# Chunk inverse of an RWKV-7 / forgetting-attention decoder layer: 104-wide products against packed 64-wide quarters of TensorE

## The chip, the cores and the metric

The kernel runs on one core of a Trainium2 chip. The metric is device time in microseconds for one execution. The kernel before took 2462.89 us, the median of three runs (2462.32 to 2469.64).

## What is computed

One decoder layer over 1040 prompt positions (16 learned ones and 1024 given) and 8 sample rows. The part that matters here is the scan of the time mixing, for 8 heads of width 64:

```python
def wkv_scan(r, decay, k, v, kk, a, state0):
    def step(state, inp):
        r_t, w_t, k_t, v_t, kk_t, a_t = inp
        s_kk = jnp.einsum('bhvk,bhk->bhv', state, kk_t)
        state = (state * w_t[:, :, None, :]
                 - s_kk[..., None] * (kk_t * a_t)[:, :, None, :]
                 + v_t[..., None] * k_t[:, :, None, :])
        return state, jnp.einsum('bhvk,bhk->bhv', state, r_t)
...
def decoder_layer(x, shift_prev, wkv0, attend, lw):
    h = rms_norm(x, lw['norm_mix'])
    u = h @ lw['w_in']
    u_r, u_f, u_g = jnp.split(u, [D_SHIFT, D_SHIFT + D_FOX_IN], axis=-1)
    o_r, new_shift, new_wkv = rwkv_time_mix(u_r, shift_prev, wkv0, lw)
    ...
    o_f = attend(q, k, v, lf)
    g_r, g_f = jnp.split(u_g, 2, axis=-1)
    merged = jax.nn.sigmoid(g_r) * (o_r @ lw['w_br_rwkv']) + jax.nn.sigmoid(g_f) * (o_f @ lw['w_br_fox'])
    x = x + merged @ lw['w_out']
    x = x + jnp.square(jax.nn.relu(rms_norm(x, lw['norm_ffn']) @ lw['w_ffn_up'])) @ lw['w_ffn_down']
```

All arithmetic is in fp32, some of the large products in two fp32r parts.

## The kernel before

The program runs these stages one after another: the projection for the time mixing (14 tiles of 128 columns), the preparation of the scan's operands, the chunk loop (314 to 1066 us), the rest of the fillers, attention, the branch and output projections, and the MLP with 2 x 32 column tiles.

The scan is done in 10 chunks of C = 104 positions, one pass of the chunk loop each, for 8 heads at once. Within a chunk the recurrence is solved by the inverse of a unit triangular 104 x 104 matrix for each head. `MB` holds the products of the chunk, masked; the inverse is built in place by doubling. Level 0 gives I - B0, where B0 is the part of `MB` between positions 2i and 2i+1; at level lv, blocks of 2^lv positions are joined into blocks of 2^(lv+1): with X the inverse so far and B the part of `MB` between the two blocks, X becomes X - X B X. The kernel holds X (`Xm`) and its transpose (`XTr`), since both stand as an operand. There are N_LV = 7 levels, 0 to 6; level 6 joins the positions below 64 to those above.

By engine, within a pass:

- GpSimd (L1935 to L1941) makes `bm_lv`, the mask of level lv times `MB`, for all heads in one operation (104 x 832), into the two buffers of `Bm` in turn.
- VectorE makes `xt_init` (L1601), the identity minus `Bm[0]`.
- TensorE transposes `XTr` (L890) into banks 0 and 1, four heads each (q = 0, 1), and ScalarE copies the result to `Xm` (L1313).
- In each level 1 to 6, for q = 0 and then q = 1: TensorE multiplies `Bm` with `Xm` (t1, L902, banks 0 and 1), ScalarE copies the result to `T1` (L1320), TensorE multiplies `XTr` with `T1` for the new `Xm` (t2, L913, banks 2 and 3; not in level 6) and `T1` with `XTr` for the new transpose (t2, L915, banks 4 and 5), and VectorE subtracts both from PSUM (L1611, L1613).
- Then TensorE goes on with `wt` (L924), `u` (L943, L947), `y` (L951, L954, L959) and the state (L963, L966), all with `XTr` or what follows from it. VectorE normalises, TensorE transposes the result (L972), and the next pass begins.

Each engine runs its own instructions in the order in which they are written; they meet in counting semaphores (`ch_pe`, `ch_act`, `ch_dve`, `ch_pool`), one step for each named result. `Filler` (L345) puts products of the later projections between these: a pass does 48 of 128 x 128 x 350, and `fill.run(n)` issues the next n of them. In each level one stands behind t1 and one behind t2, and `fill.run(2)` stands behind level 6. An fp32 matmul leaves two records in the trace, each with a weight load (LDWEIGHTS) of its own; a transpose leaves one.

The names that the change touches are `Xm`, `XTr`, `T1`, `Bm` (tiles at L492 to L497), the step lists `ch_dve` and `ch_pool` (L515, L520), and the bodies of the chunk on TensorE (L887 to L943), ScalarE (L1311 to L1320), VectorE (L1564, L1600 to L1614) and GpSimd (L1934 to L1941).

Of the kernel before, what the change touches and what calls it, by code (L numbers as in the profile page):

```python
# [129 lines left out]
def build(nc, A):  # L130
    with ExitStack() as ctx:
# [290 lines left out]
        for u in range(N_UN):  # L422
# [9 lines left out]
            if a + 1 == HN and i + 1 < HP:  # L432
# [59 lines left out]
        Xm, XTr = r_ch.take(NH, C), r_ch.take(NH, C)  # L492
# [3 lines left out]
        T1 = r_c2.take(NH, C)  # L496
        Bm = r_c2.take(NH, C), r_c2.take(NH, C)  # L497
# [20 lines left out]
                          for t in (("x", "xt") if lv < N_LV - 1 else ("xt",))]  # L518
                       + ["sum", "mean", "state_sum", "state", "center", "sq", "var", "norm"])
        ch_pool = Steps(sem("ch_pool"), [f"bm_{lv}" for lv in range(N_LV)] + ["bonus", "gate"])  # L520
# [254 lines left out]
        def _(pe):  # L775
# [59 lines left out]
            def pe_chunk(c):  # L835
# [17 lines left out]

                fill.run(16)
# [33 lines left out]
                for q in range(2):  # L888
                    for j in range(4):
                        last = pe.transpose(PS[0:C, q, j * C:(j + 1) * C], XTr[0:C, 4 * q + j], ident[0:C, 0:C])  # L890
                    ch_pe.done(last, f"x_{q}")
                for lv in LEVELS:
                    for q in range(2):
                        if q == 0:
                            pe.wait_ge(ch_pool.sem, ch_pool.after(c, f"bm_{lv}"))
# [24 lines left out]
                fill.run(2)  # L920
                wait(ch_dve, f"x_{N_LV - 1}_1_xt")
                for h in range(NH):
                    e, p = h // HP, h % HP
                    last = pe.matmul(PS[e * HD:(e + 1) * HD, 0, p * C:(p + 1) * C], An[0:C, vcols(h)],  # L924
                                     XTr[0:C, h], start=True, stop=True)
# [16 lines left out]
                for h, e, p, rows in by_rows():  # L942
                    pe.matmul(u_out(e, p), XTr[0:C, h], Zm[0:C, h * HD:(h + 1) * HD], start=(p == 0), stop=False,  # L943
# [1140 lines left out]
```

## Time and profile before

| | before |
|---|---|
| median of three runs | 2462.89 us |
| the profiled execution | 2458.04 us |
| its span, first to last instruction | 2456.2 us |
| mean granted TensorE clock | 0.972 of full |
| busy: TensorE, VectorE, ScalarE, GpSimd | 92, 38, 23, 8% |
| the chunk loop | ten passes of 74.95 us |

A row of a profile names a line of the kernel, an engine (PE is TensorE, PEld its weight loads, DVE VectorE, ACT ScalarE, POOL GpSimd, SP the engine that issues transfers), the operation and its tiles. Matmuls are pipelined: the time of one record overlaps the next, so a rate is read from starts, not from the length of one record.

### The profile page before, as it was taken

To read this page: it belongs to the slowest core of one execution; us is meant where nothing else is said; L and a number is where in the kernel's file an instruction comes from. 1 tells how busy PE (TensorE), PEld (TensorE's weight loads), DVE (VectorE), ACT (ScalarE), POOL (GpSimd) and SP (SyncE) were. 2 spreads that over 40 slices of the span, in tenths; PEclk is the share of its full clock that TensorE was granted. 3 is DMA by queue.
4 is the path that set the end of the run, shared out by engine and by line. 5 is a ranking of instruction groups with operands and counts; after the bars stand their busy time and mean duration, and the time that the engine had idled before them with its cause. 6 is when DMAs were issued, how large, how long until landed. Compare 5 with 4: busy or idle time off the path is not lost.

```text
span 2456.2 us, 37471 instructions
## 1 busy us (share of the span) xinstructions
PE 2251.5 (92%) x14718; PEld 1880.7 (77%) x14718; DVE 936.9 (38%) x1400; ACT 577.0 (23%) x913; POOL 191.0 (8%) x136
## 2 busy tenths in 40 slices
PE   2998689999999999999888899996999999999995
PEld 1996377778777788765555566666999999999995
DVE  5332644433444433433467622116322222222234
ACT  3112422222222222231334322003211211211220
POOL 0000022112221122200111000000000000000000
PEclk8999899999999999999899999998999999999998
DMA  2114621100111111156553634211111111111111
GB/s 110 44 43 109 179 85 46 45 33 13 45 45 55 46 35 45 42 142 115 193 182 124 210 118 177 78 34 43 43 52 43 43 47 47 43 43 51 43 43 70
DMA packets 108390, 184.31 MB, mean 75 GB/s; under 512 B 65070, under 2 KB 65390, under 8 KB 104966
## 3 DMA queue, kind: packets, MB, share of 16 engines
q1 hardware_dynamic: 106022, 174.95, 22.8%
q10 hardware_dynamic: 2304, 8.50, 1.4%
q8 instruction: 41, 0.67, 0.1%
q14 instruction: 23, 0.19, 0.0%
HBM read 147.71 MB, written 35.71 MB: 75 GB/s over the span
## 4 chain that ended last, share of the span: by engine, by line
PE 86%; DVE 9%; ACT 2%; issue 2%; DMA 1%; SPq 0%; ACTq 0%; DVEq 0%
PE ps L279 36%; PE ps L345 16%; PE ps L255 9%; PE ps L902 4%; PE ps L915 4%; PE ps L913 3%; PE ps L1153 2%; DVE arena L1730 2%; PE ps L1138 1%; PE ps L1125 1%; DVE arena L1596 1%; PE ps L874 1%; DVE normed L327 1%; PE ps L843 1%; PE ps L954 1%
## 5 line engine op out<-in xcount | busy, mean ns | idle before, releaser
L345 PE MATMUL ps<-normed,weights 128*128 128x350 f32 x1344 | 440.0, 468 | 8.4 <-ACTq L1265 8.3
L279 PE MATMUL ps<-h_split,w_split 128*128 128x350 f32 x2304 | 375.9, 325 | 14.7 <-DVE h_split L1883 14.7
L279 PEld LDWEIGHTS ps<-h_split,w_split 128*128 128x128 f32 x2304 | 374.0, 191 | 16.9 <-issue 12.9
L279 PE MATMUL ps<-ff_split,w_split 128*128 128x350 f32 x2304 | 371.4, 323 | 0.0
L279 PEld LDWEIGHTS ps<-ff_split,w_split 128*128 128x128 f32 x2304 | 370.9, 189 | 0.0
L345 PEld LDWEIGHTS ps<-normed,weights 128*128 128x128 f32 x1344 | 243.7, 192 | 121.3 <-issue 10.0
L1870 DVE TENSOR_TENSOR arena<-arena,ps 128x1050 f32 (+1 forms) x40 | 50.0, 1249 | 351.9 <-PE ps L279 266.5
L1941 POOL TENSOR_TENSOR arena<-arena,constants 104x832 f32<-104x832 f32 x70 | 136.2, 1952 | 580.6 <-DVE arena L1596 444.9
L255 PE MATMUL ps<-fox,weights 128*128 128x350 f32 x576 | 171.3, 457 | 3.0 <-DVE fox L1860 3.0
L255 PEld LDWEIGHTS ps<-fox,weights 128*128 128x128 f32 x576 | 109.0, 189 | 64.0 <-issue 3.6
L915 PE MATMUL ps<-arena 104*104 104x104 f32 x960 | 155.0, 255 | 0.0
L289 ACT CAST w_split<-weights 128x1024 fp32r<-128x1024 f32 x78 | 81.4, 1043 | 275.9 <-PE ps L279 245.1
L279 PE MATMUL ps<-h_high,w_split 128*128 128x350 f32 x672 | 129.5, 327 | 16.7 <-DVE h_low L1481 16.7
L913 PE MATMUL ps<-arena 104*104 104x104 f32 x800 | 138.6, 255 | 0.0
L1899 DVE TENSOR_TENSOR squares<-squares 128x1050 f32<-128x1050 f32 x32 | 40.1, 1254 | 248.5 <-ACT squares L1449 248.5
L1611 DVE TENSOR_TENSOR arena<-arena,ps 104x416 f32<-104x416 f32 x100 | 58.7, 587 | 189.5 <-PE ps L915 189.5
L279 PEld LDWEIGHTS ps<-h_high,w_split 128*128 128x128 f32 x672 | 113.0, 191 | 18.8 <-issue 13.7
L293 DVE TENSOR_TENSOR w_split<-weights,w_split 128x1024 fp32r<-128x1024 f32 x78 | 95.1, 1220 | 82.5 <-ACT w_split L289 82.5
L915 PEld LDWEIGHTS ps<-arena 104*104 104x104 f32 x960 | 121.7, 172 | 2.3
L913 PEld LDWEIGHTS ps<-arena 104*104 104x104 f32 x800 | 109.4, 172 | 11.4
L902 PEld LDWEIGHTS ps<-arena 104*104 104x104 f32 x960 | 100.4, 171 | 22.2 <-ACT arena L1313 4.5
L902 PE MATMUL ps<-arena 104*104 104x104 f32 x960 | 108.7, 260 | 2.4 <-ACT arena L1313 2.4
(255 smaller groups left out, 2314.4 us busy)
## 6 DMA issues: line engine op xcount, KB each, us to landing
weights<-in_wu SPq DMA_DIRECT2D x122, 512.0 KB, 3.5
normed<-in_vp SPq DMA_DIRECT2D x64, 260.0 KB, 4.8
normed<-in_kp SPq DMA_DIRECT2D x64, 256.0 KB, 5.3
arena<-chunk_dram SPq DMA_DIRECT2D x10, 1248.0 KB, 5.5
arena<-gate_dram SPq DMA_DIRECT2D x16, 525.0 KB, 4.7
chunk_dram<-arena SPq DMA_DIRECT2D x12, 520.0 KB, 6.7
chunk_dram<-fox SPq DMA_DIRECT2D x12, 520.0 KB, 4.2
arena<-samp_dram SPq DMA_DIRECT2D x10, 512.0 KB, 9.3
```

What stands on the lines that cost most here:

```text
L255: last = pe.matmul(PS[:, 3 * s + g, 0:G], W[:, s, k * P:(k + 1) * P], x[:, k, g * G:(g + 1) * G], start=(k == 0), stop=(k == nk - 1))
L279: last = pe.matmul(PS[:, 3 * s + g, 0:G], ws[:, s, wh, k * P:(k + 1) * P], x[xh][:, k, g * G:(g + 1) * G], start=(k == 0 and wh + xh == 0) ...
L289: act.copy(of[0][:, s, 0], W[:, s]).then_inc(w_hi[s], 1)
L293: dve.tensor_tensor(of[0][:, s, 1], W[:, s], of[0][:, s, 0], ALU.subtract).then_inc(w_split[s], 1)
L345: last = self.pe.matmul(PS[:, 6 + m % 2, 0:G], W[:, s, k * P:(k + 1) * P], HT[:, k, g * G:(g + 1) * G], start=(k == 0), stop=(k == KT - 1))
L902: last = pe.matmul(PS[0:C, q, j * C:(j + 1) * C], Bm[lv % 2][0:C, h], Xm[0:C, h], start=True, stop=True)
L913: pe.matmul(PS[0:C, 2 + q, j * C:(j + 1) * C], XTr[0:C, h], T1[0:C, h], start=True, stop=True)
L915: last = pe.matmul(PS[0:C, 4 + q, j * C:(j + 1) * C], T1[0:C, h], XTr[0:C, h], start=True, stop=True)
L1153: last = pe.matmul(PS[e * HD:(e + 1) * HD, 6, at:at + C], vnat[0:C, b, col:col + HD], PTm[0:C, u % 2, e, s0 + b], start=(b == 0), stop=(b ...
L1611: done(dve.tensor_tensor(quad(Xm, q), quad(Xm, q), PS[0:C, 2 + q, 0:4 * C], ALU.subtract), f"x_{lv}_{q}_x")
L1870: dve.tensor_tensor(dst, dst, grp(s), ALU.add).then_inc(evac[s], 1)
L1941: ch_pool.done(pool.tensor_tensor(Bm[lv % 2][0:C], MB[0:C, :, 0], mask, ALU.mult), f"bm_{lv}")
```

## The change

Each head's 104 x 104 matrices are kept as two diagonal blocks: positions 0 to 63 on partitions 0 to 63 (`top`), positions 64 to 103 on partitions 64 to 103 (`low`), both in 64 columns. The levels 1 to 5 never couple the two, so each product is made as two products of 64 rows, one on the first and one on the last quarter of TensorE's array. Level 6 makes only the block between them. The full transpose is put together in a new tile `XTF` by the last two levels. The transposes of `XTr` become products with a packed identity.

```diff
-        Xm, XTr = r_ch.take(NH, C), r_ch.take(NH, C)
+        HB, HR = 64, C - 64
+        Xm, XTr, XTF = r_ch.take(NH, HB), r_ch.take(NH, HB), r_ch.take(NH, C)
...
+        identP = r_c2.take(HB)
+        top, low = slice(0, HB), slice(HB, C)
+        half_turn = sem("half_turn")
...
+                def by_halves(bank, j, lhs, rhs, h=None):
+                    at = slice(j * HB, (j + 1) * HB)
+                    a = lhs[:, (bank % 2) * 4 + j]
+                    b = rhs if h is None else rhs[:, h]
+                    pe.matmul(PS[top, bank, at], a[top], b[top], start=True, stop=True)
+                    return pe.matmul(PS[low, bank, at], a[low, 0:HR], b[low], start=True, stop=True)
...
                 for q in range(2):
+                    if q == 0:
+                        pe.sem_inc(half_turn, 1)
                     for j in range(4):
-                        last = pe.transpose(PS[0:C, q, j * C:(j + 1) * C], XTr[0:C, 4 * q + j], ident[0:C, 0:C])
+                        last = by_halves(q, j, XTr, identP)
                     ch_pe.done(last, f"x_{q}")
-                for lv in LEVELS:
+                for lv in LEVELS[:-1]:
                     for q in range(2):
...
+                        pe.sem_inc(half_turn, 1)
                         for j in range(4):
-                            h = 4 * q + j
-                            last = pe.matmul(PS[0:C, q, j * C:(j + 1) * C], Bm[lv % 2][0:C, h], Xm[0:C, h],
-                                             start=True, stop=True)
+                            last = by_halves(q, j, Bm[lv % 2], Xm, 4 * q + j)
                         ch_pe.done(last, f"t1_{lv}_{q}")
                     fill.run(1)
                     for q in range(2):
                         wait(ch_act, f"t1_{lv}_{q}")
...
+                        pe.sem_inc(half_turn, 1)
                         for j in range(4):
                             h = 4 * q + j
-                            if lv < N_LV - 1:
-                                pe.matmul(PS[0:C, 2 + q, j * C:(j + 1) * C], XTr[0:C, h], T1[0:C, h],
+                            if lv < N_LV - 2:
+                                by_halves(2 + q, j, XTr, T1, h)
+                            else:
+                                pe.matmul(PS[top, 2 + q, j * HB:(j + 1) * HB], XTr[top, h], T1[top, h],
                                           start=True, stop=True)
-                            last = pe.matmul(PS[0:C, 4 + q, j * C:(j + 1) * C], T1[0:C, h], XTr[0:C, h],
-                                             start=True, stop=True)
+                        for j in range(4):
+                            last = by_halves(4 + q, j, T1, XTr, 4 * q + j)
                         ch_pe.done(last, f"t2_{lv}_{q}")
                     fill.run(1)
+                lv = N_LV - 1
+                for q in range(2):
+                    wait(ch_dve, f"x_{lv - 1}_{q}_x")
+                    pe.sem_inc(half_turn, 1)
+                    for j in range(4):
+                        h = 4 * q + j
+                        last = pe.matmul(PS[low, q, j * HB:(j + 1) * HB], MB[top, h, 0, low], Xm[top, h],
+                                         start=True, stop=True)
+                    ch_pe.done(last, f"t1_{lv}_{q}")
+                fill.run(1)
+                for q in range(2):
+                    wait(ch_act, f"t1_{lv}_{q}")
+                    wait(ch_dve, f"x_{lv - 1}_{q}_xl")
+                    pe.sem_inc(half_turn, 1)
+                    for j in range(4):
+                        h = 4 * q + j
+                        last = pe.matmul(PS[top, 4 + q, j * HB:j * HB + HR], T1[low, h], XTF[low, h, low],
+                                         start=True, stop=True)
+                    ch_pe.done(last, f"t2_{lv}_{q}")
+                fill.run(1)
 
                 fill.run(2)
...
-                        ch_act.done(act.copy(quad(T1, q), PS[0:C, q, 0:4 * C]), f"t1_{lv}_{q}")
+                        part = slice(0, C) if lv < N_LV - 1 else low
+                        ch_act.done(act.copy(quad(T1, q)[part], PS[part, q, 0:4 * HB]), f"t1_{lv}_{q}")
...
+            for b in Bm:
+                order(dve.memset(b[low, :, HR:HB], 0.0))
+            order(dve.memset(XTF[low, :, top], 0.0))
+            order(dve.tensor_copy(identP[top], ident[top, 0:HB]))
+            order(dve.tensor_copy(identP[low], ident[low, HB:2 * HB]))
...
                         if lv < N_LV - 1:
-                            done(dve.tensor_tensor(quad(Xm, q), quad(Xm, q), PS[0:C, 2 + q, 0:4 * C],
+                            part = slice(0, C) if lv < N_LV - 2 else top
+                            done(dve.tensor_tensor(quad(Xm, q)[part], quad(Xm, q)[part], PS[part, 2 + q, 0:4 * HB],
                                                    ALU.subtract), f"x_{lv}_{q}_x")
-                        done(dve.tensor_tensor(quad(XTr, q), quad(XTr, q), PS[0:C, 4 + q, 0:4 * C],
-                                               ALU.subtract), f"x_{lv}_{q}_xt")
+                        if lv < N_LV - 2:
+                            done(dve.tensor_tensor(quad(XTr, q), quad(XTr, q), PS[0:C, 4 + q, 0:4 * HB],
+                                                   ALU.subtract), f"x_{lv}_{q}_xt")
+                        elif lv < N_LV - 1:
+                            done(dve.tensor_tensor(XTF[top, four, top], XTr[top, four], moved(4, top, HB),
+                                                   ALU.subtract), f"x_{lv}_{q}_xt")
+                            done(dve.tensor_tensor(XTF[low, four, low], XTr[low, four, 0:HR], moved(4, low, HR),
+                                                   ALU.subtract), f"x_{lv}_{q}_xl")
+                        else:
+                            done(dve.tensor_scalar(XTF[top, four, low], moved(4, top, HR), -1.0, None, ALU.mult),
+                                 f"x_{lv}_{q}_xt")
...
-                for lv in range(N_LV):
+                for lv in range(N_LV - 1):
...
+                    for part, name in ((top, "top"), (low, "low")):
+                        n = part.stop - part.start
+                        mask = cst[part, C_LV + lv * C + part.start:C_LV + lv * C + part.stop]
+                        ch_pool.done(pool.tensor_tensor(Bm[lv % 2][part, :, 0:n], MB[part, :, 0, part],
+                                                        mask.unsqueeze(1).to_broadcast([n, NH, n]), ALU.mult),
+                                     f"bm_{lv}_{name}")
+                        pool.wait_ge(ch_pool.sem, ch_pool.after(c, f"bm_{lv}_{name}"))
```

The products `wt` and `u` read `XTF` in place of `XTr`, with the same shapes. `moved(bank, part, n)` names the first n of 64 columns of each of four heads in PSUM.

## Rows read from the trace of the kernel before

**Rows 1.** The page: busy time by engine, and the chain that ended last.

```profile
PE 2251.5 (92%) x14718; PEld 1880.7 (77%) x14718; DVE 936.9 (38%) x1400; ACT 577.0 (23%) x913; POOL 191.0 (8%) x136
...
PE 86%; DVE 9%; ACT 2%; issue 2%; DMA 1%; SPq 0%; ACTq 0%; DVEq 0%
PE ps L279 36%; PE ps L345 16%; PE ps L255 9%; PE ps L902 4%; PE ps L915 4%; PE ps L913 3%; PE ps L1153 2%; DVE arena L1730 2%; PE ps L1138 1%; PE ps L1125 1%; DVE arena L1596 1%; PE ps L874 1%; DVE normed L327 1%; PE ps L843 1%; PE ps L954 1%
```

**Rows 2.** Table by stretch: busy us (xinstructions) by engine, then granted clock, DMA share, GB/s.

```profile
690.85:765.80 74.95, 72.59 (x569) 58.42 (x567) 30.80 (x46) 18.45 (x37) 16.17 (x9) 0.98 0.11 31
713.72:749.45 35.73, 35.49 (x310) 31.23 (x309) 12.90 (x22) 7.79 (x16) 9.70 (x5) 1.00 0.04 15
...
1198.00:1400.00 202.00, 170.94 (x1713) 107.10 (x1713) 143.44 (x475) 83.55 (x207) 26.12 (x38) 0.94 0.50 169
```

**Rows 3.** Waits of TensorE, 390 to 1066 us: us in total, times, longest.

```profile
PE ps L972 <- DVE arena L1642: 18.1, 9, 2.0
...
PE ps L902 <- ACT arena L1313: 2.1, 9, 0.2
```

**Rows 4.** Chain of waits inside one level: start us, us, what.

```profile
726.52 1.67 PE ps L902 x16
728.19 0.61 PE ps L345 x2
...
731.73 0.32 PE ps L345
```

**Rows 5.** Timeline of TensorE behind the levels: start us, us, instructions.

```profile
747.57 1.95 PE L345 MATMUL ps<-normed,weights 128*128 128x350 f32 x6
749.45 1.34 PE L924 MATMUL ps<-arena 104*64 104x104 f32 x16
750.72 1.44 PE L345 MATMUL ps<-normed,weights 128*128 128x350 f32 x4
752.00 1.60 PE L943 MATMUL ps<-arena 104*104 104x64 f32 x16
753.53 0.95 PE L947 MATMUL ps<-arena 64*104 64x64 f32 x16
754.31 0.90 PE L951 MATMUL ps<-arena 64*104 64x64 f32 x16
...
759.41 0.69 PE L963 MATMUL ps<-arena 104*64 104x64 f32 x16
759.93 0.64 PE L966 MATMUL ps<-arena 104*64 104x64 f32 x16
```

**Rows 6.** Timeline: VectorE and ScalarE around one level, and two operations for size.

```profile
702.10 0.59 ACT L1302 COPY arena<-ps 104x512 f32<-104x512 f32 x1
...
725.75 0.78 PE L345 MATMUL ps<-normed,weights 128*128 128x350 f32 x2
725.95 0.59 DVE L1611 TENSOR_TENSOR arena<-arena,ps 104x416 f32<-104x416 f32 x1 [0.26 <-PE ps L915]
...
727.36 0.51 ACT L1320 COPY arena<-ps 104x416 f32<-104x416 f32 x1 [4.38 <-PE ps L902]
...
760.61 0.42 DVE L1634 TENSOR_TENSOR arena<-arena,ps 128x256 f32<-128x256 f32 x1 [0.19 <-PE ps L966]
```

**Rows 7.** Timeline where the first copy begins: GpSimd, VectorE, TensorE.

```profile
708.86 3.85 POOL L1941 TENSOR_TENSOR arena<-arena,constants 104x832 f32<-104x832 f32 x2 [13.47 <-DVE arena L1596]
...
710.83 2.75 DVE L1601 TENSOR_TENSOR arena<-constants,arena 104x832 f32<-104x832 f32 x1 [2.06 <-POOL arena L1941]
...
713.72 0.88 PE L890 MATMUL ps<-constants,arena 104*104 104x104 f32 x8
```

**Rows 8.** Timeline before the first pass: VectorE.

```profile
319.39 1.60 DVE L1578 TENSOR_TENSOR_SCAN arena<-constants,arena 128x104 f32<-128x104 f32 x4 [4.92 <-DMA arena<-chunk_dram]
```

**Rows 9.** DMA from 300 to 765 us: one queue's packets and MB; one issue's us to landing.

```profile
q8 instruction: 5, 0.08, 0.1%
...
lora_weights<-in_vp SPq DMA_DIRECT2D x48, 4.0 KB, 1.7
```

More of the change, by code:

```diff
@@ L495, in build @@
         MB = r_c2.take(NH, 2, C)
-        T1 = r_c2.take(NH, C)
-        Bm = r_c2.take(NH, C), r_c2.take(NH, C)
+        T1 = r_c2.take(NH, HB)
+        Bm = r_c2.take(NH, HB), r_c2.take(NH, HB)
+        identP = r_c2.take(HB)
+        top, low = slice(0, HB), slice(HB, C)
+        half_turn = sem("half_turn")
         Zm = r_c2.take(512)
@@ L517, in build @@
                        + [f"x_{lv}_{q}_{t}" for lv in LEVELS for q in range(2)
-                          for t in (("x", "xt") if lv < N_LV - 1 else ("xt",))]
+                          for t in (("x", "xt") if lv < N_LV - 2 else ("x", "xt", "xl") if lv < N_LV - 1 else ("xt",))]
                        + ["sum", "mean", "state_sum", "state", "center", "sq", "var", "norm"])
-        ch_pool = Steps(sem("ch_pool"), [f"bm_{lv}" for lv in range(N_LV)] + ["bonus", "gate"])
+        ch_pool = Steps(sem("ch_pool"), [f"bm_{lv}_{b}" for lv in range(N_LV - 1) for b in ("top", "low")] + ["bonus", "gate"])
         ds_pe, ds_act, ds_dve = sem("ds_pe"), sem("ds_act"), sem("ds_dve")
@@ L888, in pe_chunk @@
                 for q in range(2):
+                    if q == 0:
+                        pe.sem_inc(half_turn, 1)
                     for j in range(4):
-                        last = pe.transpose(PS[0:C, q, j * C:(j + 1) * C], XTr[0:C, 4 * q + j], ident[0:C, 0:C])
+                        last = by_halves(q, j, XTr, identP)
                     ch_pe.done(last, f"x_{q}")
-                for lv in LEVELS:
+                for lv in LEVELS[:-1]:
                     for q in range(2):
                         if q == 0:
-                            pe.wait_ge(ch_pool.sem, ch_pool.after(c, f"bm_{lv}"))
+                            pe.wait_ge(ch_pool.sem, ch_pool.after(c, f"bm_{lv}_low"))
                         if lv == 1:
@@ L924, in pe_chunk @@
                     last = pe.matmul(PS[e * HD:(e + 1) * HD, 0, p * C:(p + 1) * C], An[0:C, vcols(h)],
-                                     XTr[0:C, h], start=True, stop=True)
+                                     XTF[0:C, h], start=True, stop=True)
                 ch_pe.done(last, "wt")
@@ L942, in pe_chunk @@
                 for h, e, p, rows in by_rows():
-                    pe.matmul(u_out(e, p), XTr[0:C, h], Zm[0:C, h * HD:(h + 1) * HD], start=(p == 0), stop=False,
+                    pe.matmul(u_out(e, p), XTF[0:C, h], Zm[0:C, h * HD:(h + 1) * HD], start=(p == 0), stop=False,
                               skip_group_check=True)
@@ L1312, in act_chunk @@
                     wait(ch_pe, f"x_{q}")
-                    ch_act.done(act.copy(quad(Xm, q), PS[0:C, q, 0:4 * C]), f"x_{q}")
+                    ch_act.done(act.copy(quad(Xm, q), PS[0:C, q, 0:4 * HB]), f"x_{q}")
                 out(2)
@@ L1599, in _ @@
                             cm, ALU.mult), f"mask_{m}{i}")
-                wait(ch_pool, "bm_0")
-                done(dve.tensor_tensor(XTr[0:C], ident[0:C, 0:C].unsqueeze(1).to_broadcast([C, NH, C]),
+                wait(ch_pool, "bm_0_low")
+                done(dve.tensor_tensor(XTr[0:C], identP[0:C].unsqueeze(1).to_broadcast([C, NH, HB]),
                                        Bm[0][0:C], ALU.subtract), "xt_init")
@@ L1609, in _, with moved @@
                         wait(ch_pe, f"t2_{lv}_{q}")
+                        four = slice(4 * q, 4 * q + 4)
+                        def moved(bank, part, n):
+                            return PS[part, bank + q, 0:4 * HB].rearrange("p (a b) -> p a b", a=4)[:, :, 0:n]
                         if lv < N_LV - 1:
-                            done(dve.tensor_tensor(quad(Xm, q), quad(Xm, q), PS[0:C, 2 + q, 0:4 * C],
+                            part = slice(0, C) if lv < N_LV - 2 else top
+                            done(dve.tensor_tensor(quad(Xm, q)[part], quad(Xm, q)[part], PS[part, 2 + q, 0:4 * HB],
                                                    ALU.subtract), f"x_{lv}_{q}_x")
-                        done(dve.tensor_tensor(quad(XTr, q), quad(XTr, q), PS[0:C, 4 + q, 0:4 * C],
-                                               ALU.subtract), f"x_{lv}_{q}_xt")
+                        if lv < N_LV - 2:
[9 more added lines that the diff above has]
+                                 f"x_{lv}_{q}_xt")
                 def heads(ap):
@@ L1939, in _ @@
                         pool.wait_ge(ch_pe.sem, ch_pe.after(c, f"t1_{lv - 2}_1"))
-                    mask = cst[0:C, C_LV + lv * C:C_LV + (lv + 1) * C].unsqueeze(1).to_broadcast([C, NH, C])
-                    ch_pool.done(pool.tensor_tensor(Bm[lv % 2][0:C], MB[0:C, :, 0], mask, ALU.mult), f"bm_{lv}")
+                    for part, name in ((top, "top"), (low, "low")):
[5 more added lines that the diff above has]
+                        pool.wait_ge(ch_pool.sem, ch_pool.after(c, f"bm_{lv}_{name}"))
                 pool.wait_ge(bg_in, 16 * c + 16)
```

## The prediction

> **What bounds the kernel now.** I read the page first: of the span of 2456.2 us TensorE is busy for 92%, and of the chain that ended last 86% is TensorE; VectorE, ScalarE and GpSimd have long idle times [rows 1]. The three product lines of the chunk inverse, L902, L913 and L915, stand in that chain with 4 + 4 + 3%, some 260 us. Then the table by stretch: one pass of the chunk loop takes 74.95 us, and the stretch that the change rewrites, from the transposes of `XTr` to the `wt` products, takes 35.73 us, in which TensorE is busy for 35.49 at full granted clock [rows 2]. Then TensorE's waits over nine passes: apart from the 2 us before the last transposes of each pass it waits for almost nobody, 2.1 us in all in front of L902 [rows 3]. So in this stretch the stream of TensorE's instructions is the bound, and what is taken from the stream is taken from the time, until a wait shows.
>
> The chain of one level shows how the 5.82 us of a level are made [rows 4]: 1.67 us for the sixteen records of the t1 products (an fp32 matmul leaves two records), 0.61 for one filler matmul, then 32 records of the t2 products, from 728.80 to the next filler at 731.73, one filler more. The t2 records come every 2.93 / 32 = 92 ns, which is 0.88 ns for each of their 104 moving columns. The t1 records come every 104 ns; sixteen at 92 would be 1.47, so 0.2 us of each level is waiting already, for VectorE's two subtractions (below).
>
> The stretch holds 14 filler matmuls (2 for each of six levels, then `fill.run(2)`) at 0.61, together 8.5 us. What is the inverse's own is 35.7 - 8.5 = **27.2 us**.
>
> **The change, step by step.**
>
> *Records.* Before: 8 transposes with one record each, 96 of t1 and 176 of t2, 280 in a pass. After: each 104-wide product is two 64-wide ones. The first copy becomes 16 products (32 records); t1 in levels 1 to 5 is 5 x 16 products (160); t2 in levels 1 to 4 is 4 x 32 products (256); in level 5 it is 8 + 16 products (48); level 6 is 8 + 8 products (32). That is 528 records, of which 48 (the eight of level 5 that make only the top block, and all of level 6) lie on one quarter of the array; the other 480 alternate between two quarters.
>
> *What a quarter record costs.* No row shows a 64 x 64 tile. The nearest are in the tail of the pass [rows 5]. L963 has 64-column weights in alternating column halves and 64 moving columns: 16 records from 759.41 to 759.93, 33 ns each. L947 has alternating row halves, but 104-column weights: 16 records from 753.53 to 754.31, 49 ns. L943, full width, 104-column weights and only 64 moving columns: 1.53 / 16 = 96 ns, no less than with 104 moving columns. So loading the 104 columns takes as long as moving 104, and it is the larger of the two that sets the pace: 0.88 x 104 / 2 = 46 explains L947's 49, and 0.88 x 64 / 2 = 28 explains L963's 33. A diagonal quarter has 64 columns on both sides and differs from its neighbour in rows and columns, so it is nearest to L963: I take **33 ns**, with 30 and 50 (L947) as ends. A record on one quarter alone has no partner: 0.88 x 64 = 57 ns. 480 x 33 + 48 x 57 = 15.8 + 2.7 = 18.5 us in place of the old records.
>
> *Changes between full width and quarters.* Each filler matmul is now surrounded by quarters: 25 changes in a pass, before there were none inside a level. L924 shows both directions [rows 5]: six filler records of 302 ns from 747.57 would end at 749.38 and L924 begins at 749.45; the four fillers behind it take 1.28 instead of 1.21. So 0.07 a change, 1.7 us. Ends 0 and 0.15 (the weights of the next tile are not loaded ahead, one load is exposed).
>
> *The 25 increments of `half_turn`.* As I read the code, the wait in front of a group of quarters now sits on an instruction of the queue and not on the first product. Where the wait is over before the queue gets there they are hidden by the filler in the queue. Where it binds (the q = 1 group of t1 in each level, the two first groups of level 1, about 8 in a pass) the restart costs one more step; the trace of before has no such increment inside the stretch, the nearest is VectorE's end at 713.58 to TensorE's start at 713.72 [rows 7], so up to 0.14 each and I take 0.1: 0.8 us. Ends 0 and 25 x 0.14 = 3.5.
>
> *The waits inside a level.* t2 of q = 1 ends, 0.2 later VectorE starts (the filler behind t2 begins at 725.75, the subtraction at 725.95 [rows 6]), now two subtractions of 256 columns; 0.42 each by L1634 [rows 6] instead of 0.59, together 0.87 with the gap, then 0.14 back to TensorE: 1.21 us. Its cover is one filler and the q = 0 group of t1: 0.61 + 16 x 0.033 = 1.14. So 0.1 us of stall in each of five levels, where there was 0.2. ScalarE's copy of 256 columns (0.37, by 0.51 for 416 and 0.59 for 512 [rows 6]) has filler plus 0.5 us as cover. In level 1 the shorter groups expose the copies of x_0 and x_1 by some 0.2. Sum 0.7 us.
>
> *The last level.* It is a chain of small steps: t2 of level 5, VectorE (now three operations for each q, 0.42 + 0.42 + 0.32), t1 (0.46 for each q), copy, t2 (0.46 each), one operation, `wt`. I followed it: t1 of q = 1 is ready to start 2.99 us after the start of level 5's t2 and TensorE is at it at 3.04; its copy is back at 4.20 while TensorE has to do q = 0's t2 until 4.56; VectorE's last result is ready at 5.7 and the `wt` products come at 6.8, behind three fillers. Nothing is exposed, and 1.1 us of cover is left at the end.
>
> *GpSimd and the start of the stretch.* Masking goes in two pieces of 64 and 40 rows: (512 + 320) columns at 1.95 / 832 us [rows 7] are again 1.95, plus 0.1 or so for the wait between. `xt_init` shrinks from 2.76 to about 1.7. It ended at 713.58, just when TensorE was at its end of the fillers; it will end 0.8 us earlier. The other masks have a level (4.8 us) for 2.1 us of work. Cost nothing.
>
> *Setup.* Three memsets and two copies on VectorE before the loop, about 1.3 us. There VectorE waits 4.92 us for the first chunk to land [rows 8]. Cost nothing; without that cover 1.3 us once.
>
> *Sum for a pass.* 18.5 + 1.7 + 0.8 + 0.7 = **21.7 us** in place of 27.2: 5.5 us less, the stretch falls from 35.7 to 30.2, the pass from 75.0 to 69.4, a middle level from 5.8 to about 4.8. Nothing else in the pass changes: fillers, `wt`, tail. The weights for the fillers and the next chunk land 3 to 6 us after their issue and the pass stays far longer than that. Ten passes: 55 us. The profiled execution took 2458.04 us, 4.85 under the median of 2462.89; 2458 - 55 = 2403 for it, and from the median **2408 us**.
>
> **The rivals.**
>
> *A: the changes and increments cost nothing.* 18.5 + 0.5 us a pass, 8.2 less: 2381. For it: L924's 0.07 may be rounding of the modelled starts. 13%.
>
> *B: waits take over.* The margins in a level are 0.1 us; if each step of VectorE, ScalarE or the restart of the queue is a little longer than I take it, half a microsecond a level is exposed: 3 us a pass, gain 2.5: 2438. For it: TensorE already stalled 0.2 us a level at the slower pace. 12%.
>
> *C: the loop no longer stays in TensorE's instruction memory.* A pass has 572 records now, each with a weight load of its own, 820 after. The trace shows five fetches of instructions on queue q8 from 300 to 765 us, through six passes [rows 9]: the first pass fetches, the others run from memory. If the longer body falls out, each of the eight jumps back waits for a fetch; a small transfer takes 1.7 us to land [rows 9]. 14 us more: 2422. Against it: at the jump TensorE waits 2.0 us for VectorE anyway [rows 3], and that would hide most. 8%.
> The Trainium skill (Runtime: NRT & Kernel Launch, Instruction fetch mechanics) gives TensorE room for 2048 instructions in pages of 256. By that page 2 x 820 matmul instructions with their loads, and some 80 waits and register operations, lie over eight pages, all that there are, with none for the page ahead; by it C would come true. The trace agrees as far as the pages go: five packets are 0.08 MB, 16 KB each [rows 9].
>
> *D, the slower side: quarters that share a bank run one after another, or load as slowly as row halves.* Top and low quarter of a product write the same bank, which L947's row halves do not; L963's column halves do. The point from which the change loses is (27.2 - 2.7 - 3.2) / 480 = **44 ns** a record. At L947's 49 to 50 ns the pass is 2.7 us longer: 2490 (8%, of which 2 lie within 0.3% of no change, at 43 to 46 ns). Fully in turn, at 57 ns: 480 x 57 = 27.4, and 33.3 us a pass in place of 27.2: 2524 (4%).
> The Trainium skill (TensorEngine Tiling (Array Packing), Restrictions and Gotchas) says that different row tiles cannot access the same PSUM bank simultaneously. Read strictly, that page gives the 57 ns and the sum of 2524; L963 agrees only in that column tiles of one bank do overlap.
>
> *E: half the array idle lets the granted clock fall* from 2.4 to 1.2 GHz, and TensorE's 27 us of the new stretch double: 2408 + 270 = 2678. Against it: the attention stage, with its small tiles and 85% busy, was granted 0.94 [rows 2]. 2%.
>
> **How the numbers follow.** The forecast has 53%: 2395 to 2423, its own spread from 31 to 35 ns and 0 to 0.1 a change. A 13, B 12, C 8, D 12, E 2. A measurement of this kernel can tell about 0.3%, 7 us, from no change. Faster: 53 + 13 + 12 + 8 = 86%. Within: 2%. Slower: 6 + 4 + 2 = 12%. The range leaves out D and E (14%) and some tails: 2378 to 2446.
>
> **What would show it.** In the trace of after: the period between the t1 groups of levels 2 to 4 (5.82 before) at 4.6 to 5.0 us; sixteen records of a q group in 0.53 us; chunk starts 69.4 us apart; TensorE's waits in front of the t1 line under 0.2 us each. D shows as a group of 16 records taking 0.8 us or more, B as waits for VectorE or ScalarE inside the levels, C as more than five q8 packets in the six passes of the first loop and a gap at its head, E in the granted clock. I am wrong in the main if a quarter record costs over 44 ns, or if the 25 restarts cost far over 0.1 us each.

## The result, and the profile after

| | before | after |
|---|---|---|
| median (lowest to highest) | 2462.32 us (2456.48 to 2469.64) | 2449.17 us (2446.01 to 2450.52) |
| the profiled execution | 2458.04 us | 2450.52 us |
| its span | 2456.2 us | 2448.7 us |

The ratio of the times is 0.9944, with a 95% interval of 0.9927 to 0.9960: 13 us faster, where 55 us were forecast, and 3 us above the upper end of the forecast range. What follows shows that the change itself gained 67 us and that 54 of them were lost again at a place it doesn't touch.

The table by stretch of the kernel after, in the columns of [rows 2]: one pass of the chunk loop, the stretch from the first product with the packed identity to `wt`, one middle level, and the last pass of the first loop:

```profile
389.00:463.56 74.56, 68.29 (x820) 50.32 (x821) 25.83 (x49) 16.70 (x37) 15.72 (x15) 0.96 0.14 39
413.40:442.80 29.40, 29.30 (x558) 22.10 (x559) 9.67 (x24) 6.00 (x16) 8.50 (x8) 1.00 0.07 20
418.47:423.12 4.65, 4.65 (x101) 3.54 (x101) 1.68 (x4) 0.74 (x2) 2.12 (x2) 1.00 0.02 4
688.41:759.90 71.49, 68.77 (x820) 50.52 (x821) 22.78 (x43) 13.53 (x29) 14.23 (x13) 0.96 0.13 38
```

The stretch is where the change was made, and it fell from 35.7 us to 29.4 (30.2 was forecast), a middle level from 5.8 us to 4.65. Yet the pass is 74.56 us and was 74.95 [rows 2]. TensorE is busy 68.29 of them, so over 6 us are idle, and its granted clock is 0.96 and not 0.98. Inside the stretch the clock is 1.00. The loss is outside the stretch.

The waits of TensorE from 390 to 1056 us, in the columns of [rows 3]:

```profile
PE ps L345 <- issue: 28.9, 7, 5.0
PE ps L1009 <- DVE arena L1700: 18.1, 9, 2.0
PE ps L886 <- DVE arena L1639: 5.5, 18, 0.4
```

The second and third row are the old waits (L1009 is the transpose of the result, L972 before). The first is new: seven times TensorE waits for nothing that the profile shows, in front of a filler product (an eighth such wait lies ahead of 390 us). The chain of waits at two jumps from the end of a pass to the head of the next, and at the place where the first loop falls through to the second without a jump:

```profile
458.69 0.70 DVE arena L1700
...
459.44 0.58 PE ps L1009 x4
460.02 3.54 issue
...
759.33 0.58 PE ps L1009 x4
759.90 2.32 PE ps L345 x7
...
827.88 0.57 PE ps L1009 x4
828.46 4.97 issue
833.42 11.80 PE ps L345 x32
```

All eight jumps back have such a gap: 3.63, 3.54, 3.63, 3.59 and 3.53 us in the first loop, 4.97, 4.99 and 4.60 in the second, 32.5 us together. The fall-through has none. Nor does the kernel before have one at its jumps: L972 ends there at 390.77 and the next filler starts at 390.80.

```profile
390.19 0.58 PE L972 MATMUL ps<-constants,arena 104*128 104x104 f32 x4 [2.02 <-DVE arena L1642]
390.80 9.68 PE L345 MATMUL ps<-normed,weights 128*128 128x350 f32 x32
```

The page and the transfers of 300 to 757 us count the packets that fetch instructions:

```profile
q8 instruction: 117, 1.92, 0.3%
...
q8 instruction: 52, 0.85, 0.8%
```

117 in the whole run, where the kernel before has 41, and 52 in the first loop, where it has five [rows 9]. The transfers inside the first gap alone, 385.37 to 389.00 us:

```profile
q8 instruction: 1, 0.02, 2.2%
```

Each of the eight gaps holds one such packet of 16 KB. By narrower windows it starts at 386.00 here, 0.6 us after the transposes, and takes 1.3 us (2.2% of 16 engines' 3.63 us); TensorE starts 1.7 us after its end, and the next packet begins at 389.48, when TensorE is already running. In the second loop the packet starts 1.9 to 2.3 us after the transposes, and that makes those gaps the longer ones.

The gap costs more than its length. The timeline of TensorE's weight loads and products around the first jump:

```profile
384.79 0.38 PEld L1009 LDWEIGHTS ps<-constants,arena 104*128 104x128 f32 x4 [2.56 <-DVE arena L1700]
388.99 0.50 PEld L345 LDWEIGHTS ps<-normed,weights 128*128 128x128 f32 x2 [3.83 <-issue]
389.74 0.34 PEld L345 LDWEIGHTS ps<-normed,weights 128*128 128x128 f32 x1 [0.25 <-issue]
390.32 0.34 PEld L345 LDWEIGHTS ps<-normed,weights 128*128 128x128 f32 x1 [0.24 <-issue]
```

and the table by stretch of the head's 32 filler records:

```profile
389.00:394.00 5.00, 5.00 (x9) 3.03 (x10) 2.38 (x4) 0.00 (x0) 0.88 (x1) 0.50 0.26 51
394.00:401.14 7.14, 7.14 (x27) 4.55 (x26) 0.00 (x0) 0.45 (x1) 0.00 (x0) 1.00 0.61 209
```

Two idle stretches stand close together, 2.0 us for VectorE and then 3.6 us for instructions, and after them the granted clock is 0.50, the lower of its two levels (1.2 GHz): filler records stand 0.58 us apart and not 0.29. The 32 records take 12.14 us where they take 9.44 at full clock (experiment 1). The eight heads take 97.1 us together (11.5 to 12.6 each), which is 21.6 us more than eight of 9.44. Gaps and heads together: 32.5 + 21.6 = 54.1 us.

### The profile page after: what moved, and what is told of

Same layout as the page of the kernel before. It is cut to its first block, busy times and chain, and to the rows that moved or that the text cites. A ratio compares the mean times of both kernels' runs of the same rounds, so it can differ in the third digit from the quotient of the medians.

```text
span 2448.7 us, 42896 instructions
## 1 busy us (share of the span) xinstructions
PE 2208.9 (90%) x17198; PEld 1796.3 (73%) x17198; DVE 884.7 (36%) x1425; ACT 559.1 (23%) x913; POOL 187.6 (8%) x186
## 4 chain that ended last, share of the span: by engine, by line
PE 84%; DVE 9%; issue 3%; DMA 1%; ACT 1%; SPq 0%; ACTq 0%; DVEq 0%
PE ps L279 36%; PE ps L345 17%; PE ps L255 9%; PE ps L863 4%; PE ps L864 3%; PE ps L1190 2%; DVE arena L1788 2%; PE ps L1175 1%; PE ps L1162 1%; DVE arena L1639 1%; PE ps L886 1%; PE ps L847 1%; PE ps L991 1%; DMA weights<-in_wu 1%; PE ps L811 1%
## 5 line engine op out<-in xcount | busy, mean ns | idle before, releaser
L345 PE MATMUL ps<-normed,weights 128*128 128x350 f32 x1344 | 468.1, 491 | 43.9 <-issue 32.5
L279 PEld LDWEIGHTS ps<-h_split,w_split 128*128 128x128 f32 x2304 | 372.1, 190 | 18.7 <-issue 12.9
L345 PEld LDWEIGHTS ps<-normed,weights 128*128 128x128 f32 x1344 | 252.5, 199 | 173.9 <-issue 58.9
L863 PEld LDWEIGHTS ps<-arena 64*64 64x64 f32 x2400 | 148.6, 135 | 46.1 <-issue 46.1
L2001 POOL TENSOR_TENSOR arena<-arena,constants 64x512 f32<-64x512 f32 x120 | 132.5, 1104 | 553.5 <-DVE arena L1639 496.9
L863 PE MATMUL ps<-arena 64*64 64x64 f32 x2400 | 163.7, 220 | 1.0
L864 PE MATMUL ps<-arena 40*40 40x64 f32 x2400 | 157.9, 218 | 0.0
L864 PEld LDWEIGHTS ps<-arena 40*40 40x40 f32 x2400 | 139.2, 112 | 0.0
L1660 DVE TENSOR_TENSOR arena<-arena,ps 104x256 f32<-104x256 f32 (+1 forms) x100 | 41.9, 419 | 180.1 <-PE ps L864 173.9
L1788 DVE CUSTOM_DVE_ANT_0 arena<-ps,arena 104x416 f32<-104x416 f32 (+3 forms) x152 | 67.8, 493 | 83.8 <-PE ps L1162 83.8
L1487 ACT ACTIVATE squares<-ps 128x1050 f32<-128x1050 f32 x32 | 33.5, 1048 | 259.5 <-PE ps L279 259.5
```

Of the source, the lines that this page charges most:

```text
L279: last = pe.matmul(PS[:, 3 * s + g, 0:G], ws[:, s, wh, k * P:(k + 1) * P], x[xh][:, k, g * G:(g + 1) * G], start=(k == 0 and wh + xh == 0) ...
L345: last = self.pe.matmul(PS[:, 6 + m % 2, 0:G], W[:, s, k * P:(k + 1) * P], HT[:, k, g * G:(g + 1) * G], start=(k == 0), stop=(k == KT - 1))
L863: pe.matmul(PS[top, bank, at], a[top], b[top], start=True, stop=True)
L864: return pe.matmul(PS[low, bank, at], a[low, 0:HR], b[low], start=True, stop=True)
L1660: done(dve.tensor_tensor(quad(Xm, q)[part], quad(Xm, q)[part], PS[part, 2 + q, 0:4 * HB], ALU.subtract), f"x_{lv}_{q}_x")
L1788: dve.tensor_tensor_reduce(Sm[u % 3][0:C, e, lo:hi].rearrange("p b t -> p (b t)"), PS[0:C, 2 * (n % 2) + e, (lo - CUTS[c][0]) * C:(hi - CU ...
```

## Experiments

All ratios are to the kernel before, which ran on the same chip beside each of them.

**1 and 2. No jumps, after and before.** TensorE's two loops are written out, so that its stream has no jump. Nothing else changes:

```diff
-            with pe.Fori(0, C_FOX) as c:
-                pe_chunk(c)
-            with pe.Fori(C_FOX, NC) as c:
-                pe_chunk(c)
+            for c in range(NC):
+                pe_chunk(c)
```

> The kernel after, with TensorE's ten passes of the chunk written out one behind the other and no jump back; the work is the same. Theory F (fetch): the gap of 3.5 to 5.0 us at the head of eight passes, and the first fillers that run at the lower clock behind it (12.3 instead of 9.7 us), come from the jump back to instructions that have to be fetched again. Written out there is no jump: no gap, passes of 68 to 69 us, 2449 - 8 x 6.3 = about 2399 us, ratio to before 0.975. Rival L (the gap is a wait of the loop's end, such as draining TensorE or a transfer, or belongs to the quarters): the gap stays, and the time stays within 10 us of 2449.

> The kernel before with TensorE's passes written out in the same way. Theory F: its loop ran from instruction memory without a gap, so nothing is won: within 0.3% of 2462, passes of 75 us. If writing out helps by itself (its waits are against constants, with 56 register operations fewer in a pass), this kernel too is faster, by up to 50 us, and e1 would not show the fetch.

The kernel after without jumps: 2394.61 us, ratio 0.9726 (0.9704 to 0.9749). That is 54.6 us under the looped one, and 54.1 were counted in the trace. One pass of it, and the chain at the head of this pass:

```profile
452.60:520.92 68.32, 65.64 (x821) 48.98 (x821) 25.93 (x48) 16.68 (x37) 15.81 (x14) 1.00 0.14 42
```

```profile
452.02 0.57 PE ps L1009 x4
452.60 9.44 PE ps L345 x32
```

No gap, full clock, a pass of 68.32 us. The looped pass is this one plus its gap and its slow head: 68.32 + 3.54 + (12.14 - 9.44) = 74.56, the measured length of the first looped pass. The kernel before without jumps: 2461.44 us, ratio 0.9997 (0.9985 to 1.0009). Its jumps cost nothing, so the 54 us are not the price of jumps as such. Instruction packets alone don't decide either: written out, the kernel after fetches 96 packets and the one before 76, and neither waits for them. A stream that goes straight on is fetched ahead, a jump is not.

**3. Half the jumps.** Two passes to a turn of the loop: three jumps in place of eight, bodies twice as long.

```diff
-            with pe.Fori(0, C_FOX) as c:
-                pe_chunk(c)
+            with pe.Fori(0, C_FOX // 2) as c:
+                pe_chunk(2 * c)
+                pe_chunk(2 * c + 1)
...
```

> The kernel after with two passes in each turn of TensorE's loops: three jumps back instead of eight. Theory F: three gaps, each about as long as before, 2449 - 5 x 6.3 = about 2418 us. Rival L, if the gap belongs to each pass: 2449; if it grows with the length of the body: gaps of 7 us or more and no gain.

2413.34 us, ratio 0.9805 (0.9782 to 0.9828). Its waits have `PE ps L345 <- issue: 11.7, 3, 5.0`, and the chain at the first of the three jumps:

```profile
454.62 0.57 PE ps L1009 x4
455.19 3.51 issue
458.70 12.05 PE ps L345 x32
```

So each jump has its price, 3.2 to 5.0 us of gap and over 2 us of slow head, and three of them cost 18.7 us (2413.34 - 2394.61).

**4, 8, 9 and 10. The kernel before with a longer body.** Does length alone bring the gaps, without quarters and without `half_turn`? One-element products whose result is unused stand in front of the transposes of `yt`; all else is computed as before. A pass of TensorE has 1200 instructions before and 1722 after (an fp32 matmul is four: two records and their two weight loads).

```diff
+                for _ in range(133):
+                    pe.matmul(PS[0:1, 4, 0:1], ident[0:1, 0:1], ident[0:1, 0:1], start=True, stop=True)
                 wait(ch_dve, "norm")
```

> The kernel before with 133 matmuls of one element (266 records, 532 instructions) added ahead of the last transposes of each pass, which makes its loop as long as that of the kernel after. Theory F: gaps of 3.5 to 5 us at the head of eight passes and over 100 packets on q8, as in the kernel after, without any quarter. Rival L (the quarters or the increments cause the gap): no gap, 41 packets. The added matmuls themselves cost some 5 to 8 us a pass either way.

> The kernel before with 62 matmuls of one element in a pass (124 records, 248 instructions; e4 had 532). The loop is then about 1450 instructions long. Theory F with room for eight pages of 256, one of them for the page ahead: the loop lies over seven and stays, no gap, five packets on q8 from 300 to 765 us as before. If the room is smaller, gaps of 2.4 us and more as in e4.

> The kernel before with 85 matmuls of one element in a pass (170 records, 340 instructions, a loop of about 1540). The first loop begins some 3.8 pages of 256 instructions into TensorE's program (by the moments of the first fetches) and ends at 9.8: seven pages. Theory F with room for eight pages, one of them ahead: it stays, no gap, and so does the second loop (9.8 to 15.8). Rival: the limit is by length and under 1540: gaps at the head of both loops' passes.

> The same with 110 (220 records, 440 instructions, a loop of about 1640). The first loop goes from page 3.8 to 10.2, eight pages; the second from 10.2 to 16.6, seven pages. Theory F with whole pages: gaps at the five jumps of the first loop, none at the three of the second. Rival (the length alone decides): all eight jumps alike, with or without a gap.

| added matmuls | instructions in a pass | gaps in the first loop (5 jumps) | in the second (3) | instruction packets |
|---|---|---|---|---|
| 0 | 1200 | none | none | 41 |
| 62 | about 1450 | none | none | 43 |
| 85 | about 1540 | none | none | 43 |
| 110 | about 1640 | all, 3.55 to 3.83 us | none | 89 |
| 133 | about 1732 | all, 2.4 to 2.9 us | all, 3.0 to 3.4 us | 117 |

Length brings the gaps without any quarter: with 133 added products the kernel before has the gaps and the very 117 packets of the kernel after. (Each of the four ran once; their times hold the added products too and are not compared.) The run with 110 is the telling one: the same body waits in one loop and not in the other. The first of its gaps in the chain, and its waits:

```profile
395.11 0.88 PE ps L974 x4
395.99 3.55 issue
```

```profile
PE ps L345 <- issue: 18.5, 5, 3.8
```

The packets are 16 KB, 256 instructions [rows 9]. If the memory holds whole pages of them, what counts is how many a loop touches, and that depends on where it starts. By the moments of the first fetches the first loop starts near page 3.8 (an estimate; counted in this way, experiments 9 to 11 come out only for a start at 0.75 to 0.98 of a page). With 110 products a pass is 6.4 pages: the first loop then lies from 3.8 to 10.2 and touches eight, the second from 10.2 to 16.6 and touches seven. Eight wait, seven don't. The same counting gives seven for both loops with 85 products (6.0 pages), and eight for both with 133 (6.8) and in the kernel after (6.7). The place of a loop's start alone doesn't decide either: both loops of experiment 9 start near 0.8 of a page, as the first of experiment 10 does, and have no gap.

**11. The kernel after with its loops shifted.** This is the test that could have refuted it. The bodies, all 1722 instructions of them, stay as they are:

```diff
+            for _ in range(16):
+                pe.matmul(PS[0:1, 4, 0:1], ident[0:1, 0:1], ident[0:1, 0:1], start=True, stop=True)
             with pe.Fori(0, C_FOX) as c:
                 pe_chunk(c)
+            for _ in range(19):
+                pe.matmul(PS[0:1, 4, 0:1], ident[0:1, 0:1], ident[0:1, 0:1], start=True, stop=True)
             with pe.Fori(C_FOX, NC) as c:
                 pe_chunk(c)
```

> The changed kernel with its two loops as they are, and nothing of the loops' bodies touched: 16 matmuls of one element (64 instructions, result unused) are put on TensorE ahead of the first loop and 19 (76 instructions) between the two loops. The run of the kernel before with 110 extra matmuls a pass put the start of the first loop near page 3.8 of 256 instructions (counted in whole pages from the program's start, an estimate from the moments at which the first pages were fetched). One pass is 1722 instructions, 6.73 pages: from 3.8 it touches eight pages, from 4.1 to 10.8 seven; the second loop would then lie from 11.1 to 17.85, seven too. Theory W (what decides is how many whole pages a loop touches: seven stay, eight don't): the gaps of 3.5 to 5.0 us ahead of the fillers vanish at all eight jumps, the instruction packets fall from 117 to about 45 to 55, with at most about six in 300 to 757 us, and the time is 2449 - 54 = 2395 us, plus up to 3 for the added matmuls: 2394 to 2400, ratio to the kernel before 0.972 to 0.976. Rival V (the length of 1722 instructions by itself is too much, wherever the loop lies): gaps at all eight jumps, 117 packets, 2447 to 2453 us. In between: the start is estimated a little wrong and one of the two loops still touches eight pages: gaps at the jumps of that loop alone (five or three), 2415 to 2430 us.

2401.58 us, ratio 0.9758 (0.9738 to 0.9778), 48 us under the kernel after by 140 instructions that do nothing. The page's packets, the chain at a jump of the first loop and at one of the second, and two heads in the table by stretch:

```profile
q8 instruction: 45, 0.74, 0.1%
```

```profile
523.13 0.58 PE ps L1009 x4
523.71 9.68 PE ps L345 x32
...
800.04 0.57 PE ps L1009 x4
800.61 0.04 issue
800.65 9.68 PE ps L345 x32
```

```profile
384.86:391.00 6.14, 6.14 (x15) 3.82 (x16) 5.54 (x9) 3.17 (x8) 2.55 (x2) 0.72 0.04 16
455.15:523.71 68.56, 65.83 (x820) 48.98 (x821) 25.93 (x48) 16.70 (x37) 15.81 (x14) 1.00 0.14 41
```

No gap at any jump. The median is 1.6 us over the upper end of what was expected. In the trace three of the nine heads that follow a pass (at 384.86, 730.36 and 937.80 us) began at a lower clock and took 11.3 to 11.4 us in place of 9.68, 5 us together, though no gap was ahead of them; that was not in the expectation. The first of them is the 0.72 in the table above. TensorE had stood at its 2.0 us wait for VectorE shortly before, as it does ahead of the six heads that ran at full clock.

**6. Work queued behind the wait.** Where does the 2.0 us wait for VectorE go, which I had counted as cover? In the kernel after the transposes of `yt` are the last work of a pass. Here six fillers go behind them, so that TensorE still has queued work when the jump is reached:

```diff
-                fill.run(16)
+                fill.run(10)
...
-                fill.run()
+                fill.run(6)
                 wait(ch_dve, "norm")
                 ...
                 ch_pe.done(last, "yt")
+                fill.run()
```

ScalarE's copies of filler results move along.

> The kernel after with its loops, but the last 6 filler matmuls of each pass stand behind the last transposes, just ahead of the jump, and the head keeps 10 of its 16 (the copies of their results on ScalarE are moved to fit). The work is the same. Theory Q (the fetch begins when TensorE's queue is past the wait in front of the last transposes, so queued work behind that wait hides it): the gap of 3.5 to 5.0 us shrinks to under 1.5 us in all eight passes, the clock does not fall behind it, 2400 to 2412 us. Rival R (the fetch begins only when TensorE has run out of work, or the fetch takes what it takes): the gap stays above 3 us, and the time at 2440 to 2450 us.

2402.41 us, ratio 0.9759 (0.9730 to 0.9787), still with 117 packets. The row of its waits, and the chain across the jump:

```profile
PE ps L345 <- issue: 2.7, 3, 1.0
```

```profile
382.41 0.58 PE ps L1009 x4
382.99 11.13 PE ps L345 x32
```

The fetches are all there, but behind queued fillers they are hidden, except for up to 1.0 us at three jumps. At those three the packet of the jump itself is covered, and the packet that follows it is not quite. The clock did fall, against the expectation: in four of the nine places between two passes (two of them jumps of the first loop, as the 11.13 above, one the fall-through, one a jump of the second) the 32 records behind the transposes began at a lower clock (0.58 to 0.67) and took 10.8 to 11.1 us, with no gap ahead of them. The packet of the jump begins 1.2 us after the 2.0 us wait ends (383.58, and the transposes begin at 382.41), as in the kernel after (386.00 and 384.79). So a fetch of a jump's target starts when the queue gets to the jump, and a wait on a semaphore ahead of the jump holds the queue as well. It can't hide the fetch; work that is already queued can.

**5. Without the increments.** Experiment 1 without the `pe.sem_inc(half_turn, 1)` lines. The semaphore is waited for by nobody.

> e1_after_unrolled without the 25 increments of half_turn in a pass. My prediction charged 0.8 us a pass for them: theory P, 8 us less than e1 (2387). Rival Z: they lie under the fillers and cost nothing, within 2 us of e1 (2395).

2394.32 us, ratio 0.9724 (0.9702 to 0.9746), against 0.9726 with them, and a pass of 68.32 us in both. They cost nothing, where the prediction had 0.8 us a pass.

**7. Fewer changes of width.** Experiment 1 with both fillers of levels 1 to 5 behind t2, so that the quarters of t1 and t2 stand together:

```diff
                         ch_pe.done(last, f"t1_{lv}_{q}")
-                    fill.run(1)
...
                         ch_pe.done(last, f"t2_{lv}_{q}")
-                    fill.run(1)
+                    fill.run(2)
```

> e1_after_unrolled with both filler matmuls of levels 1 to 5 behind t2, none behind t1: 10 changes between full width and quarters fewer in a pass. A change costs 0.09 us by the fillers' 0.79 instead of 0.61: 0.9 us less a pass. Against that t2 of q = 0 waits for ScalarE's copy, covered only by t1 of q = 1: 0.7 less 0.5 us, 0.2 in each of five levels, 1.0 us more. Theory: within 3 us of e1. If changes cost more than the fillers show, up to 10 us faster; if the wait is longer, slower by over 5 us.

2393.78 us, ratio 0.9717 (0.9695 to 0.9739): the fastest measured, but the same as experiment 1 within the intervals. Most of what the saved changes give, the new waits take:

```profile
414.99 1.37 PE ps L345 x4
...
417.10 0.38 ACT arena L1355
```

```profile
PE ps L863 <- ACT arena L1355: 4.8, 27, 0.2
```

Four filler records take 1.37 us together, and 2 x 0.79 = 1.58 when they stand apart; for it TensorE now waits for ScalarE's copy of `T1`, 4.8 us in nine passes and 1.6 more in front of L928 (level 5). The saving would be 9.4 us over these passes (five times 0.21 in each); where the rest of it went was not found.

## Why the prediction was wrong, step by step

**The gain inside the stretch: right, a little larger than summed.** With both kernels written out, the pass fell from 74.75 us (experiment 2) to 68.32 (experiment 1), by 6.4; the sum had 5.5. The terms, one by one, from the chain of waits of the kernel after inside level 2 and at the last level:

```profile
418.47 0.79 PE ps L345 x2
419.26 0.18 PE ps L863
...
420.33 0.79 PE ps L345 x2
...
423.12 0.79 PE ps L345 x2
...
437.85 1.01 PE ps L942 x16
438.87 0.79 PE ps L345 x2
439.65 1.05 PE ps L952 x16
```

- *480 quarter records.* Between the fillers at 418.47 and 420.33 lie the 32 records of t1: 420.33 - 419.26 = 1.07 us, 33 ns each. Between 420.33 + 0.79 and 423.12 lie the 64 of t2: 2.00 us, 31 ns each. 33 were taken: right, and 0.4 us a pass too much.
- *48 single records.* L942 and L952 take 63 and 66 ns each and not 57: 0.4 us a pass too little.
- *25 changes.* A filler between quarters takes 0.79 us and took 0.61 [rows 4], 0.18 for two changes: 0.09 each and not 0.07. 0.5 us too little.
- *25 increments.* Nothing (experiment 5): 0.8 us too much.
- *Waits inside a level.* In the middle levels there are none. VectorE's two subtractions for q = 1, in the timeline below, end at 423.69 + 0.42 = 424.11. TensorE needs them after the filler and t1 of q = 0, at 423.12 + 0.79 + 16 x 0.033 = 424.44: the longer filler is cover, where the prediction was 0.1 us short. Most of its 0.7 us was too much.
- *The last level.* Followed rightly: no wait stands in front of L942, L952 or `wt`.

Added up, 0.4 - 0.4 - 0.5 + 0.8 and at most 0.7 give a gain of 5.8 to 6.5 us, where 6.4 was measured.

```profile
423.24 0.42 DVE L1660 TENSOR_TENSOR arena<-arena,ps 104x256 f32<-104x256 f32 x1
423.69 0.42 DVE L1663 TENSOR_TENSOR arena<-arena,ps 104x256 f32<-104x256 f32 x1
```

Neither of the signs by which the prediction would have been "wrong in the main" came: a quarter record costs 31 to 33 ns and not 44, and the increments cost nothing. With C not coming true, the prediction's 2408 us would have stood against 2394.61, and rival A's 2381 just as far on the other side.

**The failed step: rival C, its chance and its price.** The prediction named the mechanism, and its sign (more than five packets in the first loop, a gap at its head) is what the trace showed, 52 packets and eight gaps. It gave it 8% and 14 us; it came true and cost 54. Three things in that paragraph failed.

- *The cover.* "At the jump TensorE waits 2.0 us for VectorE anyway [rows 3], and that would hide most." It hid nothing: the wait is ahead of the jump, and the fetch starts behind it (in the kernel after TensorE's 2.0 us wait and the 3.6 us gap stand one after the other; experiment 6 hides the gap with work, not with a wait). This step made the rival look harmless.
- *The size.* A 4 KB transfer of 1.7 us was taken as the price of a fetch. A gap is 3.5 to 5.0 us: its one packet takes 0.9 to 1.3 us, but 0.6 to 2.3 us pass from the transposes to the packet, and another 1.6 to 1.8 from its end to TensorE's start.
- *What follows a gap.* The clock was its own rival (E), tied to idle quarters of the array. They leave it at 1.00 in the stretch. The clock was lower instead behind every one of the eight gaps, and that is 21.6 of the 54 us. C and E were priced as if independent.

The counting was there too. The Trainium skill (Runtime: NRT & Kernel Launch, Instruction fetch mechanics) gave room for 2048 instructions in pages of 256, and the prediction said that by this page C would come true, and then set that aside in favour of the cover. Experiments 4 and 8 to 11 agree with the prediction's reading of it, eight pages with one of them for the page ahead: seven pages stay, eight don't. The same section of the Trainium skill says that a taken branch whose target isn't in the current window of two pages waits until the target page is fetched. The wait is seen here, at 3.5 to 5.0 us, but not the two pages: the kernel before jumps back over 1200 instructions, 4.7 pages, with no gap, and no packet comes at its jumps.

**The other rivals.** B: refuted in the middle levels (TensorE's waits have no line inside them). D: refuted. The top and the low quarter write the same bank, on other partitions, and overlap: single records on one quarter take 63 to 66 ns, pairs of records in quarters 62 to 66 ns for two. The rule of the Trainium skill (TensorEngine Tiling (Array Packing), Restrictions and Gotchas) that row tiles cannot access one PSUM bank at the same time would have made the pass 6 us longer; these records don't agree with it for quarters that differ in rows and columns. E: refuted as told, though the clock did matter elsewhere.

## What to carry to other kernels

When a change adds instructions to an engine's loop, count the loop's instructions before and after, in whole pages of 256 from where the loop starts, and look for instruction packets inside the loop: here seven pages of 256 stayed and eight did not, and 140 idle instructions ahead of the loops were worth 48 us. A wait ahead of a jump is no cover for what the jump needs; only work already queued behind the wait is. And price a gap together with the clock after it: a gap of 3.5 us cost 6.2 us.

## What was not expected of the hardware

- The fetch of a jump's target is not made ahead, not even while the engine stands at a wait just before the jump; fetches of a straight stream are (96 packets with no gap in experiment 1).
- Gaps are longer in the second loop (4.6 to 5.0 us) than in the first (3.5 to 3.6), since their packet starts later; they are shorter in experiment 4 (2.4 to 2.9 and 3.0 to 3.4). Why the packet starts later was not tried.
- In experiment 10, inside the padded products, TensorE also stood still up to 1.1 us at places that are no jumps (`PE ps L971 <- issue: 5.9, 6, 1.1`): perhaps one-element products run off faster than their instructions arrive; no run tests this.
- Why some heads began at the lower clock although no gap was ahead of them is open: three of nine in experiment 11, four of nine in experiment 6, one of nine in the kernel before (at 690.65 us, 10.98 us for its 32 records) and none in experiment 1.
